# Keys and values of the memory for the second layer, made between that layer's norms instead of before the first layer

## The reference

```python
for l in range(2):
    h = rmsnorm(x, norm_pre[l])
    (hq, hf_f, hf_b, hi, hz, ca, cb, cz, sb, sc, sv, sz,
     aq, ak, av, az, mq, mz) = split_cols(h @ w_in[l])
    ...                                          # branches hg, cf, sc, at
    mem_kv = rmsnorm(mem, mem_norm[l]) @ w_mem_kv[l]
    y_mem = memory_cross_attention(mq, mem_kv) * jax.nn.silu(mz)
    merged = sum(sigmoid(h @ w_gate[l, n]) * (yb @ w_branch[l, n]) for n, yb in ...)
    x = x + rmsnorm(merged @ w_out[l], norm_post[l])
```

## Time and profile before

| | |
|---|---|
| median of 3 runs | 1655.47 us (1652.59 to 1657.47) |
| the profiled execution | 1650.54 us |
| its span | 1648.7 us |
| PE busy | 1553.2 us, 94% |
| DVE busy | 1144.8 us, 69% |
| ACT busy | 828.0 us, 50% |
| mean granted PE clock | 0.972 |

### The profile page before, as it was taken

The page is one execution under the profiler, slowest core; times in us unless marked ns, Lnnn a source line. Parts: engine busy times, 40 slices in busy tenths (PEclk is TensorE's granted clock), DMA queues, the critical chain, the costliest instruction groups (busy, mean ns, idle before and its releaser), DMA issues. The chain is left out here.

```text
span 1648.7 us, 31569 instructions
## 1 busy us (share of the span) xinstructions
PE 1553.2 (94%) x12768; PEld 1482.2 (90%) x12768; DVE 1144.8 (69%) x2162; ACT 828.0 (50%) x1509; POOL 58.1 (4%) x60
## 2 busy tenths in 40 slices
PE   6999799999999998899999988999999798999997
PEld 4888799999988987899999988999999698998997
DVE  5654657787635556578997677877777669777874
ACT  3553445555434543456665564464454644644453
POOL 1000002000010000010001010000000100000000
PEclk8999899999999999999999999999999899999999
DMA  9654255566667442255555543344445332533430
GB/s 393 259 179 173 110 204 213 201 245 245 242 258 280 159 176 81 77 197 188 182 184 197 205 150 107 131 177 145 138 154 191 142 130 104 202 140 130 167 129 26
DMA packets 42047, 288.87 MB, mean 175 GB/s; under 512 B 4624, under 2 KB 6672, under 8 KB 7472
## 3 DMA queue, kind: packets, MB, share of 16 engines
q1 hardware_dynamic: 38880, 280.83, 46.5%
q10 hardware_dynamic: 3024, 6.03, 1.0%
HBM read 284.75 MB, written 2.10 MB: 174 GB/s over the span
## 5 line engine op out<-in xcount | busy, mean ns | idle before, releaser
L1935 DVE TENSOR_TENSOR w_lo<-ring,w_hi 128x1024 fp32r<-128x1024 f32 x436 | 526.9, 1230 | 297.3 <-ACT w_hi L1586 296.0
L1293 PE MATMUL bank<-h_hi,w_hi 128*128 128x256 f32 x2256 | 639.2, 291 | 10.9 <-ACT h_hi L1651 3.7
L1294 PE MATMUL bank<-h_hi,w_lo 128*128 128x256 f32 x2256 | 628.5, 286 | 0.0
L1299 PE MATMUL bank<-h_lo,w_hi 128*128 128x256 f32 x2256 | 581.1, 286 | 0.0
L1586 ACT ACTIVATE w_hi<-ring 128x1024 fp32r<-128x1024 f32 x436 | 447.7, 1053 | 115.8 <-PE bank L1299 115.2
L1293 PEld LDWEIGHTS bank<-h_hi,w_hi 128*128 128x128 f32 x2256 | 440.3, 195 | 24.8 <-issue 16.8
L1294 PEld LDWEIGHTS bank<-h_hi,w_lo 128*128 128x128 f32 x2256 | 440.3, 195 | 0.5 <-issue 0.5
L1299 PEld LDWEIGHTS bank<-h_lo,w_hi 128*128 128x128 f32 x2256 | 411.6, 195 | 0.3 <-DVE h_lo L1940 0.2
L1293 PE MATMUL bank<-a_hi,w_hi 128*128 128x256 f32 x352 | 99.4, 282 | 0.0
L1294 PE MATMUL bank<-a_hi,w_lo 128*128 128x256 f32 x352 | 98.2, 279 | 0.0
L1299 PE MATMUL bank<-a_lo,w_hi 128*128 128x256 f32 x352 | 98.2, 279 | 0.0
(11 more groups left out here) (334 smaller groups left out, 2390.5 us busy)
## 6 DMA issues: line engine op xcount, KB each, us to landing
ring<-weights SPq DMA_DIRECT2D x266, 1024.0 KB, 4.9
pos_bias<-scratch ACTq DMA_DIRECT2D x4, 512.0 KB, 6.2
x<-x_t ACTq DMA_DIRECT2D x1, 1024.0 KB, 6.4
scratch<-line ACTq DMA_DIRECT2D x1, 1024.0 KB, 8.3
mem_x<-mem_t ACTq DMA_DIRECT2D x1, 1024.0 KB, 6.5
out_t<-x SPq DMA_DIRECT2D x2, 512.0 KB, 2.6
co<-const SPq DMA_DIRECT2D x1, 462.0 KB, 6.9
levels_f<-levels ACTq DMA_DIRECT2D x1, 448.0 KB, 13.2
```

Of the source, the lines that this page charges most:

```text
L1293: pe.matmul(to, WH[:, b % SPLIT, o, :], hi[:, k, :], start=(i == 0), stop=False)
L1294: pe.matmul(to, WL[:, b % SPLIT, o, :], hi[:, k, :], start=False, stop=False)
L1299: last = pe.matmul(to, WH[:, b % SPLIT, o, :], lo[:, k, :], start=False, stop=(i == n - 1))
L1935: ve.tensor_tensor(WL[:, b % SPLIT], ring_half(b), WH[:, b % SPLIT].bitcast(F32), ALU.subtract).then_inc(w_lo_v, 1)
```

## The change

The second memory norm is no longer made between the blocks. In layer 0, before its last gates, ACT loads the memory's rows once more into another buffer (`mem_second`), together with the root, which was written to DRAM (`mem_root`) when it was made. The norm with layer 1's gain (`mem_again`) is done after the third tile of `w_out_2` has been taken. The keys of layer 1 are made between the root of z and the squares of x, the values between the root of x and mq. Between the blocks, the first key tile of layer 0 stays ahead of the root of x, and the second goes behind it. Plan and engines, cut to their core:

```diff
-    kv_taken = [[st.ps for st in p.together([fm("p2", k0[j], what="mk", j=j, l=0, src="mem") for j in range(2)])]]
+    kv_taken = [[fm("p2", k0[0], what="mk", j=0, l=0, src="mem").ps]]
     norm("final", None, "x", x_stats, l=0)
+    kv_taken[0].append(fm("p2", k0[1], what="mk", j=1, l=0, src="mem").ps)
     kv_taken[0] += token_tiles(v0, 2, what="mv", l=0, src="mem")
     first = stats([("xn", k + 1) for k in range(KD)], "x")
     p.add("load_bias", l=0, after=None)
-    norm("mem2", None, "mem", -1, rooted=True, l=1)
     norm("gain", None, "x", first, l=0)
-    k1, v1 = two("w_mem_kv_2", 1, 0), two("w_mem_kv_2", 1, BW)
-    kv_taken.append([st.ps for st in p.together([fm("p2", k1[j], what="mk", j=j, l=1, src="mem") for j in range(2)])])
-    kv_taken[1] += token_tiles(v1, 2, what="mv", l=1, src="mem")
...
     for l in range(L2):
         if l:
+            k1, v1 = two("w_mem_kv_2", l, 0), two("w_mem_kv_2", l, BW)
+            kv_taken.append([fm("p2", k1[j], what="mk", j=j, l=l, src="mem").ps for j in range(2)])
             norm("gain", x_after, src="x", l=l)
+            kv_taken[l] += token_tiles(v1, 2, what="mv", l=l, src="mem")
...
         zend(l)
+        if l + 1 < L2:
+            p.add("load_mem", l=l + 1)
         gates("hg", l)
...
         def out2(j):
             wos.append(fm("wo2", wo[j], j=j, l=l, i=p.counts["norm"] - 1))
+            if j == 2 and l + 1 < L2:
+                norm("mem_again", None, "mem_again", -1, rooted=True, l=l + 1)
             return wos[j].ps
...
+        mem2 = place("mem_second", [P, KD, S], 56320)
+        M2L = place("mem_second_lo", [P, KD, S], 56320, F32R)
+        M2H = place("mem_second_hi", [P, KD, S], 34816, F32R)
+        rsqm2 = place("rsq_mem_second", [P, S], 43008)
...
+            def load_mem(st):
+                act.dma_start(mem2[:], mem_t).then_inc(mem_again_in, 16)
+                act.dma_start(rsqm2[:], mem_root.ap()).then_inc(mem_again_in, 16)
+
             def norm(st):
+                if st.mode == "mem":
+                    act.wait_ge(rsq_ready, st.i + 1)
+                    act.dma_start(mem_root.ap(), rsqm[:]).then_inc(mem_root_out, 16)
...
                     act.wait_ge(x_norm, KD)
+                    act.wait_ge(mem_root_out, 16)
...
                     own.wait()
+                    if st.mode == "mem_again":
+                        ve.wait_ge(mem_again_in, 32)
```

More of the change, by code:

```diff
@@ L292, in norm @@
             gap_mod()
-        hn = p.count("h_norm") if kind in ("mod", "gain", "mem", "mem2") else None
+        hn = p.count("h_norm") if kind in ("mod", "gain", "mem", "mem_again") else None
         p.add("norm", mode=kind, i=i, hn=hn, src=src, **more)
@@ L502, in token_tiles @@
     def token_tiles(tiles, n, **more):
-        us = []
         for t in range(NT):
@@ L507, in token_tiles @@
                   pair=tiles[0][0][0], n=n, q=0, **more)
-            us.append(b)
-        return us
+            yield b
     k0, v0 = two("w_mem_kv_2", 0, 0), two("w_mem_kv_2", 0, BW)
-    kv_taken = [[st.ps for st in p.together([fm("p2", k0[j], what="mk", j=j, l=0, src="mem") for j in range(2)])]]
+    kv_taken = [[fm("p2", k0[0], what="mk", j=0, l=0, src="mem").ps]]
     norm("final", None, "x", x_stats, l=0)
+    kv_taken[0].append(fm("p2", k0[1], what="mk", j=1, l=0, src="mem").ps)
     kv_taken[0] += token_tiles(v0, 2, what="mv", l=0, src="mem")
@@ L600, in plan2 @@
         ak = [fm("p2", t["ak"][j], what="ak", j=j, l=l, src="h").ps for j in range(2)]
-        av = token_tiles(t["av"], 1, what="av", l=l, src="h")
+        av = list(token_tiles(t["av"], 1, what="av", l=l, src="h"))
         conv()
@@ L633, in plan2 @@
         p.add("hgscan", l=l)
-        hv = token_tiles(u[4:6], 2, what="hv", l=l, src="h")
+        hv = list(token_tiles(u[4:6], 2, what="hv", l=l, src="h"))
         sc_taken = []
@@ L913, with program @@
 KV = KD - POOL_KT
-def program(nc, weights, small, const, levels, buckets, far, x_t, mem_t, pos, scratch, out):
+def program(nc, weights, small, const, levels, buckets, far, x_t, mem_t, pos, scratch, mem_root, out):
     p = schedule()
@@ L1103, in program @@
         mem_in = sem("mem_in")
+        mem_root_out = sem("mem_root_out")
+        mem_again_in = sem("mem_again_in")
         lb_diff = sem("lb_diff_ready")
@@ L1198, in src_of @@
         def src_of(name):
-            return {"x": x, "mem": memt, "z": macc}[name]
+            return {"x": x, "mem": memt, "mem_again": mem2, "z": macc}[name]
         Lb2 = [hb[:, 0:4, :], hb[:, 4:8, :]]
@@ L1211, in output_of @@
                 return hb, XH, XL, rsqm, lambda k: (ss(("mnorm", 0), k), None)
-            return memt, YH, YL, rsqm, lambda k: (ss(("mnorm", 1), k), None)
+            return mem2, M2H, M2L, rsqm2, lambda k: (ss(("mnorm", 1), k), None)
         def logits_of(st):
@@ L1492, in p2 @@
             def p2(st):
-                hi, lo = (XH, XL) if st.src == "h" or st.l == 0 else (YH, YL)
+                hi, lo = (XH, XL) if st.src == "h" or st.l == 0 else (M2H, M2L)
                 if tiles := tiles_of(st):
@@ L1498, in tm @@
                 if st.what == "mv" and st.l:
-                    token_major(st, YH, YL)
+                    token_major(st, M2H, M2L)
                 else:
@@ L1906, in _ @@
                       qkf=qkf, gate1=gate1,
-                      ex=ex, tp=tp, ot=ot, y1=y1, wo1=wo1, up=up, upend=upend, load_bias=load_bias, p2=p2, cb=cb, hf=hf, z=z,
+                      ex=ex, tp=tp, ot=ot, y1=y1, wo1=wo1, up=up, upend=upend, load_mem=load_mem, load_bias=load_bias, p2=p2, cb=cb, hf=hf, z=z,
                       zend=zend, gate2=gate2, br=br, m2end=m2end, wo2=wo2, lnsum=lnsum, lnend=lnend, hgf=hgf, hgscan=hgscan,
@@ L2595 @@
     scratch = nc.dram_tensor("scratch", (P, 4, 512), F32, kind="Internal")
+    mem_root = nc.dram_tensor("mem_root", (P, S), F32, kind="Internal")
     out = nc.dram_tensor("out_t", (P, KD, S), F32, kind="ExternalOutput").ap()
-    program(nc, *aps, scratch, out)
+    program(nc, *aps, scratch, mem_root, out)
     r = run_bass_kernel_spmd(nc, [{n: arrays[n] for n in INPUTS}], core_ids=[0])
```

## The result

The changed kernel is slower. Its median is 1662.25 us (20 runs, 1654.38 to 1665.81), that of the kernel before on the same chips 1653.88 us (20 runs); the ratio is 1.0047 with a 95% interval from 1.0035 to 1.0060, or +7.8 us (5.8 to 9.9). The forecast was +4.1 us, the bound for slower 0.3%. So sign and range held, while the size was about half. The outcome held likeliest, a difference within 0.3% (0.57), did not come; 0.47% is on the slower side, which had 0.36.

A forecast was written before the change was run, and what follows sets the result against it. PE was taken as the bound, busy 1553.2 of 1648.7 us, its work unchanged, so only waits and clock could matter. -5.5 between the blocks and +9.6 between the layers made +4.1 us: 1659.6 us, range 1653.5 to 1664.0.

The forecast's parts named there:

- Part 1: Between the blocks: without the second memory norm and layer 1's 96 matmuls, mq is taken out 5.5 us earlier.
- Part 2: Second load, issued before layer 0's last gates: hidden beside 37 us of matmuls, costing nothing.
- Part 3: Memory norm in layer 0's output product: ACT's queue is nearly full, so last square and Ln come 6.1 us late.
- Part 4: Keys and values in the pauses between the layers: root of x ends 8.6 us late, mq is out 9.6 us late.
- the norm hides: Output product: ACT's delay at the last square is under about 1 us; net -4.6 us, chance 0.10.
- the rival on the load: Second load holds up weights, or the move changes nothing on balance: within 2 us of zero, chance 0.04.
- The clock holds: Between the layers: keys run at full speed though ACT's queue is late; 0 to +2.5 us, chance 0.16.
- the clock falls after both new pauses: Between the layers: half the clock after each pause around the keys; +5 to +7 us, chance 0.22.
- The inference from lag: Root of x between the layers: clock falls only midway, since it earlier fell 5.5 us after PE stopped; ends 8.6 us late.

The follow-up runs named there:

- kernel 3: Kernel before without the second memory norm and layer 1's keys and values (layer 1 uses layer 0's): 0.9967, -5.5 us.
- kernel 1: Kernel before with only the second load of memory rows and root, and DVE's wait for it: 1.0002, +0.3 us.
- kernel 2: Kernel before plus the load and an unused memory norm in layer 0's output product; keys and values unmoved: 1.0034, +5.6 us.
- kernel 9: Kernel before with squares of x between the blocks ahead of the splitting, no table load there, nothing moved: 0.9999, -0.2 us.
- kernel 7: Changed kernel with the norm in layer 0's last gates and squares ahead of splitting between the layers: 0.9985, -2.5 us against the kernel before.
- kernel 4: Changed kernel with the second memory norm moved into the first half of layer 0's last gates: 1.0007, +1.2 us against the kernel before.
- 5: Changed kernel with squares of x ahead of splitting between the layers and no table load there: 1.0011, +1.8 us against the kernel before.
- kernel 8: As kernel 7, with squares ahead of splitting and no table load between the blocks too: 0.9944, -9.3 us against the kernel before.
- 10: As kernel 8, with layer 0's second value step behind the root of x; half the memory values wrongly made from x: 0.9967, -5.5 us.
- kernel 6: Changed kernel plus 24 unused matmuls on PE between the keys and the root of x: 1.0019, +3.1 us against the kernel before.

## Why the prediction came out as it did

Against the first square of the output product (C) or layer 0's values (A), the steps were:

| step of the prediction | forecast | measured |
|---|---|---|
| Part 1, between the blocks | -5.5 | -3.9 (kernel 3: -4.0) |
| Part 2, the load | 0 | +0.3 (kernel 1) |
| Part 3, Ln of z late by | 6.1 | 6.55 (kernel 2: 6.56) |
| Part 4, Ln of z to first square of x | 9.5 | 9.1 |
| first square to end of root x | 3.9 | 7.1 |
| end of root x to mq out | 12.4 | 11.4 |
| Parts 3 and 4 together | +9.6 | +11.8 |
| all | +4.1 | +7.4 in A+B+C (B: -0.4), +7.8 by the ratio |

**The mechanism was right but for the clock.** The two pauses around the keys, the queue on ACT, the one split and the table load ahead of the squares, and the missing pause before mq stand in the profile where the prediction put them. The rival *the norm hides* fell with the row at 1291.44 and with kernel 2, and the rival on the load with kernel 1. *The clock holds* fell with the window of 1309 to 1315.6.

**The step that failed is the one on the clock in Part 4**: "Since this pause is short (2.6 us) and the clock fell 5.5 us after PE had stopped at 1305.3, I place the fall in the middle". The pause was 3.24 us, the clock fell inside it (0.83 in its window), and the root ran nearly all at half: 7.1 us from first square to last sum, and not 3.9. This is the rival *the clock falls after both new pauses*, to which I gave 0.22 and +5 to +7 us; its sum had mq 11.3 us late, and it was 11.8. The Trainium skill ("TensorE: Matmul & The Clock Gate", HAM oscillation) tells of bursts shorter than the waits between them, each starting cold. The trace agrees that work behind a wait starts at the lower clock, but not in the shape: the keys ahead of this wait of 3.24 us took 6.5 us. The inference from lag was the mistake. Of the pauses of 5.09, 4.18 and 3.24 us before 16 such matmuls none left the clock up, and the time behind them doesn't follow their length:

| pause | root of x, 16 matmuls |
|---|---|
| 5.09 us (kernel 2: 5.13) | 5.82 (before), 5.89 (1), 5.93 (2), 5.27 (3), 5.19 (9) |
| 4.18 or 4.19 | 5.38 (before and 2), 6.21 (1), 6.40 (changed), 6.33 to 6.45 (3 to 7) |
| 3.24 | 6.50 (changed), 5.38 (4) |
| 0.87 | 3.69 (5 and 7 between the layers, 9 between the blocks, 8 and 10 at both places) |
| 0.37 | 3.69 (kernel 6) |

**Part 1 was mis-sized by the clock too.** I took the root of x with the clock of the earlier trace rows and mq with that between the layers. Measured, the root took 6.4 us where it had 5.4, and Ln to mq 12.0 where I had 11.37: 1.6 us together. The pause ahead of this root is the same 4.18 us. All of kernels 3 to 7 have the slow root, and A is 22.5 to 22.7 in them; `mem2` is gone there beside the root. But kernel 1, where `mem2` stands as ever, has 6.21 us too, while kernel 2 has 5.38. So no cause is shown for the 1.0 us of the root, and it may be chance of the execution: against kernel 1's A of 27.31 the changed kernel saves 4.7 us, not 3.9.

**Part 3 was near for the right reason but with two errors in it.** The norm took 7.3 us (1284.25, DVE's first value, to 1291.54), not 6.25, so the fourth square came 8.5 us late and not 7.7, counted from the first. Of this the last squares made up 1.9 us and not 1.6. DVE and POOL delay each other there, which is told below; in the gates (kernel 4) the same norm takes 6.25 us.

**Part 4's other terms.** The keys were taken out 6.5 us after the end of root z where I had 7.2 for them; split and table behind them took the 2.6 us that I had put. The Trainium skill ("ScalarE: Activation LUTs", What ACT_TABLE_LOAD costs) adds a drain of 1.38 us to a switch to a different set. The load between keys and squares is no such switch, since the set is there already, so the prediction was wrong to price it by that sentence; no drain follows it either: it ends at 1308.50, and the square starts at 1308.52. The load in the output product is a switch, from the gates' `Tanh`, and shows no drain:

```profile
1280.09 1.28 ACT L1614 ACT_TABLE_LOAD   x1
1281.38 0.38 ACT L1876 ACTIVATE h_val<-bank 128x256 f32<-128x256 f32 x1
```

Here the measurement differs from the page. The 12.4 us from root x to mq were 1.0 too many: from 1315.6 to 1327.0 the granted clock is 1.00, so values and mq ran wholly at 2.4 GHz.

**What stays open.** Why a pause of 5.09 us is followed by 5.2 us of root in one kernel and 5.8 in another, and one of 3.24 by 5.4 or 6.5, isn't settled; the runs only show that pauses of 0.37 and 0.87 us left the clock up, and none between 0.87 and 3.24 us was made. The 2 to 3 us by which B is longer with the norm in the gates were traced to two waits of PE, the first of which goes with the late load; neither an earlier load nor a better place was tried.

## What to carry to other kernels

Filling one engine's pause with moved work pays only if the work's own preparation has room on the other engines: here 11.5 us of PE's work could be hidden (kernel 7), but the norm that feeds it, put into a stretch where ACT had under 2 us of slack, cost 6.6 us, more than the move gained. In a queue that is worked in order, what is urgent (the squares that a chain waits for) goes ahead of what is only due later (splitting, a table that is loaded already); 3.3 us of order were worth 7 here, because the shorter pause also kept the clock. A move can make room for a better order: squares first gained 7.1 us between the blocks after the move (kernel 8 against 7) and 0.9 before it (kernel 9), so try the order again once the work has moved.

## What the runs showed of the hardware

A pause of 0.87 us left TensorE at 2.4 GHz and one of 3.24 us did not, at a cost of 2.8 us on 16 matmuls (1.7 in kernel 4); 24 useless matmuls in the pause bought this back (kernel 6).

ACT's table load took 1.28 us, and the next operation started 0.02 us behind it, also where the set had to be changed.

VectorE and GpSimd slow each other. In the changed kernel DVE's and POOL's timelines show, in the output product:

```profile
1287.29 0.41 DVE L1957 TENSOR_TENSOR mem_second_lo<-mem_second,mem_second_hi 128x256 fp32r<-128x256 f32 x1
...
1289.24 0.96 DVE L1957 TENSOR_TENSOR mem_second_lo<-mem_second,mem_second_hi 128x256 fp32r<-128x256 f32 x1
```

```profile
1288.99 0.92 POOL L1201 TENSOR_TENSOR mean<-h_val 128x256 f32<-128x256 f32 x1
```

The same subtraction takes 0.41 us with POOL idle and 0.96 us when POOL's `TENSOR_TENSOR` began 0.25 us ahead of it; it ends 0.29 us after that one. The Trainium skill ("SBUF — State Buffer", Who interferes with whom) speaks of one port pair that these two engines hold by turns, exclusively; these rows agree with it. A second such meeting follows at 1290.12 (0.96 us where the same form took 0.47 at 1287.62). Together they make the 1.04 us by which the norm is longer in the product than in the gates, where POOL does only its own slice of it.
